# Hybrid GLA/RWKV-7/mLSTM block: a direction's two low-rank products in opposite row halves of TensorE, issued in couples

## The reference, cut to what matters

```python
def prep(p, grid):
    p = p + (quad_shift(p, grid[0], grid[1]) - p) * mu
    r, k, v, g, wl_f, wl_b, al_f, al_b = split_cols(p, RWKV_SIZES)   # 4 x 512, then 4 x 64 columns
    rh, vh = to_heads(r, RWKV_HEADS), to_heads(v, RWKV_HEADS)
    kk = to_heads(k * k_k, RWKV_HEADS)
    kk = kk * rsqrt(max(sum(square(kk), -1), 1e-24))

    def direction(w_lr, w0, ww2, a_lr, a0, wa2):
        w = exp(-RWKV_DECAY_SCALE * sigmoid(w0 + tanh(w_lr) @ ww2))   # rank 64
        a = sigmoid(a0 + a_lr @ wa2)                                  # rank 64
        kh = to_heads(k * (1.0 + (a - 1.0) * k_a), RWKV_HEADS)
        bonus = sum(rh * kh * rk, -1) * vh
        ...
```

## Time and profile before

| | before |
|---|---|
| three runs, us | 2903.33, 2911.9, 2916.92 |
| profiled execution, us | 2909.42 |
| its span, us | 2907.6 |
| mean granted TensorE clock | 0.922 |
| busy: PE, VectorE, ScalarE, GpSimd | 2505.9, 1625.3, 918.4, 786.4 us |

### The profile page before, as it was taken

How to read it: one execution, slowest core, us unless ns; L and a number is a source line. 1 busy time by engine, 2 the same in 40 slices (tenths; PEclk the granted TensorE clock), 3 DMA queues, 4 the chain that set the end, 5 groups by cost and what they waited for, 6 DMA issues and landing times. The chain is left out here.

```text
span 2907.6 us, 56618 instructions
## 1 busy us (share of the span) xinstructions
PE 2505.9 (86%) x24270; PEld 2129.0 (73%) x24270; DVE 1625.3 (56%) x2534; ACT 918.4 (32%) x1488; POOL 786.4 (27%) x745
## 2 busy tenths in 40 slices
PE   6899999987989884675978999999699999996986
PEld 2577776666877873554766888788599999996865
DVE  3037787644555635883585665665545656564233
ACT  2113243321232235552213333333343434340311
POOL 1111111107666533120313222222222222121421
PEclk8899999997999985777988999999899999998998
DMA  7612445644424413121562444444624343412521
GB/s 270 241 52 85 138 135 147 194 144 146 125 66 124 121 46 92 48 57 41 182 127 86 155 164 161 166 153 151 241 99 164 109 160 125 145 59 77 201 91 60
DMA packets 338281, 374.11 MB, mean 129 GB/s; under 512 B 111279, under 2 KB 274742, under 8 KB 335470
## 3 DMA queue, kind: packets, MB, share of 16 engines
q1 hardware_dynamic: 337024, 367.15, 39.2%
q10 hardware_dynamic: 1006, 3.33, 0.3%
HBM read 230.60 MB, written 139.82 MB: 127 GB/s over the span
## 5 line engine op out<-in xcount | busy, mean ns | idle before, releaser
L3321 PE MATMUL PS<-V_hi,weights_hi 128*128 128x258 f32 x832 | 237.8, 286 | 10.4 <-DVE H L3532 6.9
L469 PE MATMUL PS<-hT_hi,w_in_hi 128*128 128x512 f32 (+1 forms) x640 | 239.6, 374 | 4.7 <-DVE q_out L3120 4.7
L3322 PE MATMUL PS<-V_lo,weights_hi 128*128 128x258 f32 x832 | 236.7, 285 | 0.0
L471 PE MATMUL PS<-hT_hi,w_in_lo 128*128 128x512 f32 (+1 forms) x640 | 236.4, 369 | 0.0
L470 PE MATMUL PS<-hT_lo,w_in_hi 128*128 128x512 f32 (+1 forms) x640 | 236.3, 369 | 0.0
L3323 PE MATMUL PS<-V_hi,weights_lo 128*128 128x258 f32 x832 | 235.8, 283 | 0.0
L469 PE MATMUL PS<-h_hi,w_in_hi 128*128 128x512 f32 (+1 forms) x624 | 230.2, 369 | 5.6 <-PEq L115 3.6
L3429 POOL TENSOR_TENSOR weights_lo<-weights,weights_hi 128x1664 fp32r<-128x1664 f32 x32 | 122.0, 3813 | 412.6 <-ACT weights_hi L3381 412.6
L470 PE MATMUL PS<-h_lo,w_in_hi 128*128 128x512 f32 (+1 forms) x624 | 225.9, 362 | 0.0
L471 PE MATMUL PS<-h_hi,w_in_lo 128*128 128x512 f32 (+1 forms) x624 | 225.6, 362 | 0.0
L3293 PE MATMUL PS<-Q_hi,K_hi 128*128 128x256 f32 x640 | 184.7, 289 | 29.2 <-DMA K_lo<-kl_d 13.9
(11 more groups left out here) (462 smaller groups left out, 6348.6 us busy)
## 6 DMA issues: line engine op xcount, KB each, us to landing
chunk_in<-in_d SPq DMA_DIRECT2D x40, 512.0 KB, 3.4
w_in<-in_e_w_in_dram SPq DMA_DIRECT2D x30, 512.0 KB, 5.2
xnew<-in_o_w_in_dram SPq DMA_DIRECT2D x30, 512.0 KB, 6.2
in_d<-xnat SPq DMA_DIRECT2D x20, 640.0 KB, 6.0
modw<-in_mod_w_dram SPq DMA_DIRECT2D x12, 1024.0 KB, 9.5
xnat<-in_mod_w_dram SPq DMA_DIRECT2D x8, 1536.0 KB, 7.3
v_d<-xnew SPq DMA_DIRECT2D x16, 640.0 KB, 3.0
kh_d<-k_hi SPq DMA_DIRECT2D x16, 640.0 KB, 2.9
```

The lines of the kernel that those rows point to most:

```text
L469: pe.matmul(PS[:, bank + off // 512, 0:n], wh[:, k], hh[:, k, t], start=(k == 0), stop=False)
L471: last = pe.matmul(PS[:, bank + off // 512, 0:n], wl[:, k], hh[:, k, t], start=False, stop=(k == KT - 1))
L3321: pe.matmul(out, wh, VH[:, j, q], start=(j == seen[0]), stop=False)
L3322: pe.matmul(out, wh, VL[:, j, q], start=False, stop=False)
```

## The change

The two products of a direction get opposite halves of the partitions, and so of TensorE's rows: w of direction d stays in rows 64d to 64d + 63, a of direction d moves to rows 64(1 - d) on. For that the `a_lr` columns of the projection, their row of `mu`, and the loads of `ww2` and `wa2` are placed accordingly (`half_of`; one DMA becomes two for the columns of tile 1, and one becomes three for the parameter rows). In the table, piece i of w and of a are now issued as a couple behind piece i of the tile: couples 0 and 1 have 512 tokens, couple 2 has 256. blk1, bonus and ksum stay behind the same pieces of the projection, after the couple. ScalarE takes the sigmoids in the couples' order. Nothing is left out of the computation.

```diff
 for _p in range(4):
     _b = PREP_AT + PREP_TILES * _p
-    PREP_PE[_b, 0], PREP_PE[_b, 1] = [("w0", _p)], [("a0", _p)] + ([("blk1", _p - 1)] if _p else [])
-    PREP_PE[_b, 2] = [("bonus", _p - 1)] if _p else []
-    PREP_PE[_b + 1, 0], PREP_PE[_b + 1, 1], PREP_PE[_b + 1, 2] = [("w1", _p)], [("a1", _p)], [("ksum", _p)]
-    PREP_PE[_b + 4, 1] = [("blk0", _p)]
+    for _d in range(2):
+        for _i in range(3):
+            PREP_PE[_b + _d, _i] = [(f"w{_d}", _p, _i), (f"a{_d}", _p, _i)]
+    if _p:
+        PREP_PE[_b, 1] += prep_all("blk1", _p - 1)
+        PREP_PE[_b, 2] += prep_all("bonus", _p - 1)
+    PREP_PE[_b + 1, 2] += prep_all("ksum", _p)
+    PREP_PE[_b + 4, 1] = prep_all("blk0", _p)
...
+        def half_of(i, d):
+            return d if i == 0 else 1 - d
...
-                            sp.dma_start(wab[64 * d:64 * d + 64, i], A.p[x + "fb"[d]][0][:, p * P:(p + 1) * P]).then_inc(s["lr_in"], 16)
+                            q = 64 * half_of(i, d)
+                            sp.dma_start(wab[q:q + 64, i], A.p[x + "fb"[d]][0][:, p * P:(p + 1) * P]).then_inc(s["lr_in"], 16)
...
+                def prep_product(name, p, i):
+                    x, bank = piece_of(name, p, i)
+                    t, m = pieces(i)
+                    bank_free(x)
+                    if name[0] in "wa":
+                        j = "wa".index(name[0])
+                        at = 64 * half_of(j, int(name[1]))
+                        q = slice(at, at + 64)
+                        ins = pe.matmul(PS[:, bank, 0:m], wab[q, j], (LW, LA)[j][q, t], start=True, stop=True)
...
-                    for name, dst, j in ((f"w{d}", sg[d], J_W0 + d), (f"a{d}", aa[d], J_A0 + d)):
-                        for i in range(3):
+                    for i in range(3):
+                        t, m = pieces(i)
+                        for name, dst, j in ((f"w{d}", sg[d], J_W0 + d), (f"a{d}", aa[d], J_A0 + d)):
                             x, bank = piece_of(name, p, i)
-                            t, m = pieces(i)
```

More of the change, by code:

```diff
@@ L343, in _ @@
                               A.p[name][0, at:at + 512].rearrange("(i n) -> i n", n=P)).then_inc(s["rows_in"], 16)
-            act.dma_start(rows[V_MULR:V_MULR + 2, 0, :],
-                          A.p["rwkv_mu"][0, 2048:2304].rearrange("(i n) -> i n", n=P)).then_inc(s["rows_in"], 16)
+            act.dma_start(rows[V_MULR:V_MULR + 1, 0, :], A.p["rwkv_mu"][0:1, 2048:2176]).then_inc(s["rows_in"], 16)
+            for d in range(2):
+                act.dma_start(rows[V_MULR + 1:V_MULR + 2, 0, 64 * (1 - d):64 * (1 - d) + 64],
+                              A.p["rwkv_mu"][0:1, 2176 + 64 * d:2240 + 64 * d]).then_inc(s["rows_in"], 16)
             for d, name in enumerate(("gla_ba_f", "gla_ba_b")):
@@ L522, with prep_all @@
 PREP_PE = {}
+def prep_all(name, p):
+    return [(name, p, i) for i in range(2 if name[0:3] == "blk" else 3)]
 for _p in range(4):
     _b = PREP_AT + PREP_TILES * _p
-    PREP_PE[_b, 0], PREP_PE[_b, 1] = [("w0", _p)], [("a0", _p)] + ([("blk1", _p - 1)] if _p else [])
-    PREP_PE[_b, 2] = [("bonus", _p - 1)] if _p else []
-    PREP_PE[_b + 1, 0], PREP_PE[_b + 1, 1], PREP_PE[_b + 1, 2] = [("w1", _p)], [("a1", _p)], [("ksum", _p)]
-    PREP_PE[_b + 4, 1] = [("blk0", _p)]
-PREP_PE[PREP_AT + 4 * PREP_TILES, 1] = [("blk1", 3)]
-PREP_PE[PREP_AT + 4 * PREP_TILES, 2] = [("bonus", 3)]
-PREP_SEQ = [(name, p, i) for key in sorted(PREP_PE) for name, p in PREP_PE[key] for i in range(2 if name[0:3] == "blk" else 3)]
+    for _d in range(2):
[6 more added lines that the diff above has]
+    PREP_PE[_b + 4, 1] = prep_all("blk0", _p)
+PREP_PE[PREP_AT + 4 * PREP_TILES, 1] = prep_all("blk1", 3)
+PREP_PE[PREP_AT + 4 * PREP_TILES, 2] = prep_all("bonus", 3)
+PREP_SEQ = [x for key in sorted(PREP_PE) for x in PREP_PE[key]]
 BY_ACT = [x for x in PREP_SEQ if x[0][0] in "wa"]
@@ L579, in _ @@
                 sp.wait_ge(s["lo_pool"], 2 + n)
-                sp.dma_start(w[:, n], win[:, :, TILES0[n][2]:TILES0[n][2] + P]).then_inc(w_in[n], 16)
+                if n == 0:
+                    sp.dma_start(w[:, 0], win[:, :, RWL:RWL + P]).then_inc(w_in[0], 16)
+                else:
+                    for d in range(2):
+                        sp.dma_start(w[:, 1, :, 64 * (1 - d):64 * (1 - d) + 64], win[:, :, RAL + 64 * d:RAL + 64 * d + 64]).then_inc(w_in[1], 16)
             for m in range(NCH):
@@ L590, in _ @@
                 sp.wait_ge(v_out[i], 16 * (NCH // 2))
-                sp.wait_ge(w_in[i], 32)
+                sp.wait_ge(w_in[i], 32 if i == 0 else 64)
             sp.wait_ge(s["small"], 16 * (GROUPS4 + 1))
@@ L845, in bank_free, with block_product @@
                             pe.wait_ge(s["by_dve"], BY_DVE.index(before) + 1)
-                def block_product(p, d):
+                def block_product(p, d, h):
                     ops = (aa[0], sg[0]) if d == 0 else (sg[1], kk)
[L850 to L859, removed]
@@ L861, in prep_product @@
-                def prep_product(name, p):
-                    for i in range(3):
-                        x, bank = piece_of(name, p, i)
-                        t, m = pieces(i)
[L865 to L869, removed]
-                                            start=True, stop=True)
-                        else:
-                            ins = pe.matmul(PS[:, bank, 0:m], G.c("heads"), khs[:, t], start=True, stop=True)
-                        ins.then_inc(s["pp_ps"], 1)
+                    x, bank = piece_of(f"blk{d}", p, h)
@@ new lines, in block_product @@
+                    bank_free(x)
+                    q = slice(64 * h, 64 * h + 64)
+                    for c in range(NCH):
+                        for k in range(4):
+                            t = slice(c * CH + 32 * k, c * CH + 32 * k + 32)
+                            ins = pe.matmul(PS[32 * k:32 * k + 32, bank, 32 * c:32 * c + 32], ops[0][q, t], ops[1][q, t],
+                                            start=True, stop=True)
+                    ins.then_inc(s["pp_ps"], 1)
+                def prep_product(name, p, i):
+                    x, bank = piece_of(name, p, i)
+                    t, m = pieces(i)
+                    bank_free(x)
+                    if name[0] in "wa":
[3 more added lines that the diff above has]
+                        ins = pe.matmul(PS[:, bank, 0:m], wab[q, j], (LW, LA)[j][q, t], start=True, stop=True)
+                    else:
+                        ins = pe.matmul(PS[:, bank, 0:m], G.c("heads"), khs[:, t], start=True, stop=True)
+                    ins.then_inc(s["pp_ps"], 1)
@@ L884, in _ @@
                             ins.then_inc(s["prod"], 1)
-                        for name, p in PREP_PE.get((n, i), []):
-                            if name == "w0":
+                        for name, p, j in PREP_PE.get((n, i), []):
+                            if name == "w0" and j == 0:
                                 pe.wait_ge(s["lr_in"], 64 * (p + 1))
```

20 lines of the change are left out of this document (10 added, 10 removed).

## The result

The changed kernel takes 2919.6 us (median; 2913.4 to 2927.5), the kernel before 2911.7 in the same comparison (2903.3 to 2923.2): the ratio is 1.0023, 95% interval 1.0012 to 1.0033. That is within the 0.5% that the prediction calls no change, on the slow side of 1, and 3.6 us above the 2916 predicted. The profiled spans are 2913.3 and 2907.6 us, a difference of 5.7; at the end of the stage the changed kernel is 6.7 us behind.

The account below looks back on a forecast made before the run. TensorE was taken to set the pace in the preparation of the pairs. Terms -1.4 - 6.2 + 2.3 + 2.1 + 6.9 + 2.3 = +6 on 2909.4 gave 2915.4, stated as 2916 us; range 2902 to 2930.

Parts of the forecast that it names:

- Visits: TensorE's visits to low-rank products: a couple of 512 costs 1.25 us instead of 2.72 per visit; table-load waits go.
- ksum's chain: At ksum's third piece: a1's later third piece delays sigmoid, decay and read; 10.1 us from the 256-column piece instead of 6.07.
- GpSimd's part: In pairs 1 to 3 GpSimd runs within VectorE's decay and stops its scans: 2.3 us each, 6.9 in all.
- Gains that do not arrive: At blk1's masking, couple 2 of pairs 2 and 3 waits for DMAs: w0 and a0's gain lost, about 1.2 us added.
- The sum: Moves at each pair's ksum third piece, with GpSimd +6.9 and clock +2.3, together +6 us.
- Clock: Behind ksum's longer waits TensorE's granted clock falls: 0 to 4.5 us, of which half, 2.3, was taken.
- rival 4: Clock falls behind every longer wait and at couple 2 in pairs 2 and 3: 2921; 0.62 together with the forecast.
- Rival 1: In the decay, GpSimd does not stop VectorE's scans and the clock holds: about 2906 to 2910 us; chance 0.22.
- rival 2: Couples run one pass after the other: 2921 us by the program-order rule, 2926 to 2928 wholly serial; chance 0.11.
- Rival 3: The visits' gain arrives, VectorE and DMAs move up, ksum's wait stays: 28 us less, 2881; chance 0.05.

Follow-up runs that it names:

- same-half kernel: Changed kernel with both products of a couple in direction d's row half, order unchanged: 2932.1 us, ratio 1.0067 to the kernel before.
- early couple 2: Changed kernel with couple 2 issued behind projection piece 1, with couple 1, instead of behind piece 2: 2905.4 us, ratio 0.9972 to the kernel before.
- two buffers: A masked-block buffer for each direction: 2916.9 us on the changed kernel alone, 2894.0 added to late ksum, 2891.1 added to early couple 2.
- late ksum: Changed kernel with ksum's three pieces issued one projection piece later, behind piece 0 of the following tile: 2900.4 us, ratio 0.9964 to the kernel before.
- two fastest kernels: Changed kernel with a masked-block buffer for each direction, plus early couple 2 (2891.1 us) or late ksum (2894.0 us); both ratios 0.9937 to the kernel before.
- couple 2 early and two buffers: Changed kernel with couple 2 behind projection piece 1 and a masked-block buffer for each direction: 2891.1 us, ratio 0.9937 to the kernel before.
- mixed: Changed kernel with couple 2 of direction 1 behind projection piece 1, direction 0 unchanged, and a masked-block buffer for each direction: 2897.7 us, ratio 0.9950.

## Why the prediction was right, point by point

- **Visits.** 1.25 us as predicted, and the same-half kernel shows that the halves do it. The waits for the table load are gone; in their place ksum, bonus and blk1 wait 5.6 us more for sigmoids. By passes the trace differs from the rule of the Trainium skill weighed in the prediction ("TensorE: Matmul & The Clock Gate", Part 3, The mechanism): a's first pass (246.64) stands ahead of w's second (247.16), while in the same-half kernel both passes of w come first. By whole products the order of that rule holds: w starts and ends 0.01 us ahead of a.
- **ksum's chain.** Predicted 10.1 us from the 256-column piece and 2.3 for GpSimd, 12.4; measured 12.21. The early couple 2 takes it back to 6.74, so the cause is shown. GpSimd's part is 2.1, seen by taking it out. The Trainium skill ("SBUF — State Buffer", Who interferes with whom) has a VectorE instruction with two SBUF inputs contend with a GpSimd instruction that reads SBUF; scans of two SBUF operands obey that here, 5.37 against 3.27 us.
- **Gains that do not arrive.** That the masking's DMAs hold gains back is shown by the two buffers: they bring blk0 6.1 us forward on top of late ksum, and 7.5 on top of the early couple 2. But the step was mis-read in part. It said that couple 2 of pairs 2 and 3 ends at the DMAs. In pair 2 it waited 6.7 us, of which the runs give 2.7 to the DMAs and 4.0 to VectorE's own work ahead of the masking. In pair 3 it did not wait at all, and the bonus of the earlier trace rows that stood there, at 554.16, shows no wait either. TensorE was late itself, through a gap of 3.4 us inside blk1 (545.50 to 548.88; 2.4 before) that the trace puts down to nothing, and started couple 2 at 554.15. The DMAs were close behind all the same:

```profile
552.81 0.89 DVE L1039 TENSOR_TENSOR blocks_out<-PS,cst_pair 128x320 f32<-128x320 f32 x2 [13.69 <-DMA blk_d<-blocks_out]
```

In pair 2 couple 2 started 0.55 us behind the start of the masking, so without the gap pair 3's could have started at some 553.4, less than 1 us earlier (an estimate).

- **The sum.** ksum's third piece moved, pair by pair, by -1.55, -5.00, +0.44 and +4.54 us. The sum with GpSimd and without clock was -1.4, -5.3, -0.7 and +3.7 (it has +2.1 for pair 3, where its own terms give +2.3). The measured moves hold the clock lost in the pairs before, 3.4 us by pair 3; without it the last would be some +1.1. So the pairs themselves came out 2.6 us better than the sum, 1.8 of it in pair 3.
- **Clock.** The term that was mis-sized: 2.3 us predicted, half of a full price; the projection behind the four waits lost 4.9, or 2.6 more. That is the first half of rival 4, which had 2921. Its second half did not come: behind couple 2 the clock was 0.73 in pair 2, where it had been 0.78 before, and 1.00 in pair 3 as before.

The two misses cancel, so that blk0 came out at +6.4 where the sum had +6 is luck; that the chain and GpSimd eat the visits' gain is not, since these terms were measured as predicted. The profiled executions, on which the sum was built, differ by 5.8 us (2915.19 and 2909.42); by the medians of the runs rival 4's 2921 is a little nearer than 2916. Rival 1 fell by the scans, rival 2 by the couples' starts. Rival 3, the gain that arrives, was not this kernel; the two fastest kernels come near it, 2891 to 2894, where the visits' full gain would give 2881.

## What to carry to other kernels

Before a product that feeds a chain is moved for a better packing on TensorE, ask which wait ends the chain that it starts; here it paid to leave the feeding product early (couple 2 early), or to move the waiting end as far as the feeding one (ksum late). When a local saving, here 28 us by the prediction, shows nothing, list the waits that grew; here two edits of a line or a few beside the change turned 1.0023 into 0.9937. And an experiment that removes one named wait can leave most of it, when the engine that waited was late anyway.

## What the runs showed of the hardware that was not expected

- Two fp32 products in opposite row halves interleave pass by pass (246.63, 246.64, 247.16, 247.17), each pair of passes in about the time of one. Where the second product had a wait of its own they did not: it started 0.58 us behind the first (371.30 and 371.88 in the kernel with couple 2 early and two buffers).
- GpSimd beside VectorE's scans stretches ten of them from 3.27 to 5.37 us, nearly by GpSimd's own 2.34. One scan alone bears it: the one that starts at 377.56, behind GpSimd's start, takes 2.50 us, the other nine about 0.40.
- In the changed kernel TensorE's idle times of 4.1 to 5.8 us at ksum are followed by 7 us at a mean granted clock of 0.71 to 0.85, that is partly at 1.2 instead of 2.4 GHz; those of 1.2 to 1.9 us in pairs 1 to 3 of the couple-2-early kernel are followed by 1.00. The length of the wait alone does not settle it: in pair 0 an idle time of 2.1 us (kernel before) and one of 3.0 (couple 2 early) were followed by 0.85 and 0.76, and one of 3.6 (mixed) by 1.00. What decides there stays open.
- TensorE stands 2.4 to 5 us, from one start to the next, inside a block's run of small products, at the same two places in every kernel here (blk0 of pair 0, four records before its end, and blk1 of pair 2), with nothing in the trace that releases it. What it is stays open.
